# Softmax difference in the turned blocks instead of on VectorE, and unpadded queries

## The reference, cut to what matters

```python
def diff_attn(q, k, v, q_pos, k_pos, rel_bias, lam):
    ...
    a = probs(q[..., :DA_HEAD_DIM], k[..., :DA_HEAD_DIM]) - lam * probs(q[..., DA_HEAD_DIM:], k[..., DA_HEAD_DIM:])
    return jnp.einsum('bhqk,bkhd->bqhd', a.astype(v.dtype), v)

def peer(xn, w_q, sub_keys, u_tab, v_tab):
    ...
        act = jax.nn.gelu(jnp.einsum('td,thkd->thk', xb, u_tab[eidx]).astype(jnp.float32), approximate=False)
        return jnp.einsum('thk,thkd->td', (g * act).astype(xb.dtype), v_tab[eidx])
```

## Time and profile before

| | |
|---|---|
| median of 3 runs | 4118.31 us (4114.87 to 4126.76) |
| the profiled execution's own time | 4114.87 us |
| its span | 4113.1 us |
| PE / DVE / POOL / ACT busy | 68% / 62% / 55% / 26% |
| mean granted clock of PE | 0.748 of full speed |
| DMA, mean over the span | 338 GB/s |

### The profile page before, as it was taken

How to read it: one execution, slowest core, us unless ns; L and a number is a source line. 1 busy time by engine, 2 the same in 40 slices (tenths; PEclk the granted TensorE clock), 3 DMA queues, 4 the chain that set the end, 5 groups by cost and what they waited for, 6 DMA issues and landing times.

```text
span 4113.1 us, 50105 instructions
## 1 busy us (share of the span) xinstructions
PE 2803.7 (68%) x17164; PEld 1458.7 (35%) x17164; DVE 2543.0 (62%) x6861; ACT 1058.1 (26%) x2882; POOL 2270.1 (55%) x2365
## 2 busy tenths in 40 slices
PE   7889998677477757684768477758874754333365
PEld 6745544334243424342433243324442421000011
DVE  2445756766786677658776777688767556644400
ACT  3312212322232233222332233233322111110121
POOL 1102443665666566556666666566656656666665
PEclk9989999787678767786778678868875576555567
DMA  7635898999999999999999999999999999999998
GB/s 206 193 124 186 268 336 273 380 371 367 348 372 357 366 369 358 328 359 345 357 371 368 362 359 381 360 370 369 382 358 357 377 348 354 363 366 370 359 365 313
DMA packets 544250, 1389.51 MB, mean 338 GB/s; under 512 B 59496, under 2 KB 223776, under 8 KB 544000
## 3 DMA queue, kind: packets, MB, share of 16 engines
q0 software_dynamic: 335024, 1215.35, 79.0%
q1 hardware_dynamic: 196752, 161.33, 12.3%
q10 hardware_dynamic: 12224, 9.63, 0.8%
HBM read 1352.93 MB, written 33.04 MB: 337 GB/s over the span
## 4 chain that ended last, share of the span: by engine, by line
PE 16%; issue 14%; DMA 13%; POOL 11%; another core or an unknown queue 8%; DVE 7%; ACT 2%; SPq 1%; ACTq 0%; DVEq 0%; POOLq 0%
DMA d_vb<-in_peer_v_dram,d_eidT 6%; POOL d_vb L1686 5%; POOL d_ub L1667 5%; PE d_pY L1716 5%; DVE d_ub L1880 3%; DMA d_ub<-in_peer_u_dram,d_eid 2%; PE d_pS L842 2%; DMA r_side<-out_v_sample_dram 2%; PE r_pB L1432 2%; PE r_pB L1605 1%; PE d_pS L908 1%; PE d_pS L928 1%; DMA r_side<-scratch_hgT 1%; DMA t_shared<-scratch_kT 1%
## 5 line engine op out<-in xcount | busy, mean ns | idle before, releaser
L1880 DVE CUSTOM_DVE_ANT_0 d_ub<-d_ub,d_pX 128x1024 f32<-128x1024 f32 x1024 | 1240.7, 1217 | 630.1 <-DMA d_ub<-in_peer_u_dram,d_eid 516.0
L1667 POOL DMA_INDIRECT d_ub<-in_peer_u_dram,d_eid x1152 | 1133.8, 984 | 887.1 <-DVE d_hdot L1880 402.3
L1686 POOL DMA_INDIRECT d_vb<-in_peer_v_dram,d_eidT x1096 | 1053.5, 961 | 816.0 <-PE d_pY L1716 347.4
L1716 PE MATMUL d_pY<-d_vb,d_dg 128*32 128x256 f32 x8768 | 934.3, 514 | 829.4 <-DMA d_vb<-in_peer_v_dram,d_eidT 565.8
L1716 PEld LDWEIGHTS d_pY<-d_vb,d_dg 128*32 128x32 f32 x8768 | 260.1, 129 | 1405.3 <-issue 1197.4
L1755 ACT ACTIVATE d_dg<-c_late_sb,d_wgtT 128x32 f32<-128x32 f32 x1152 | 336.1, 315 | 1352.8 <-PE d_pY L1716 851.0
L704 PE MATMUL d_pX<-d_wq,d_vb 128*128 128x512 f32 (+3 forms) x1536 | 469.1, 458 | 16.0 <-DMA d_vb<-in_w_in_dram 8.5
L704 PEld LDWEIGHTS d_pX<-d_wq,d_vb 128*128 128x128 f32 x1536 | 269.4, 199 | 179.3 <-issue 112.2
L842 PE MATMUL d_pS<-t_shared,t_qz 128*128 128x512 f32 (+3 forms) x384 | 209.9, 680 | 52.9 <-DMA t_shared<-scratch_kT 31.9
L1880 DVE CUSTOM_DVE_ANT_0 d_ub<-d_ub,d_vb 128x1024 f32<-128x1024 f32 x128 | 155.4, 1221 | 44.6 <-DMA d_ub<-in_peer_u_dram,d_eid 43.8
L1432 PE MATMUL r_pB<-r_side,c_small_sb 128*128 128x128 f32 (+15 forms) x1152 | 170.5, 314 | 17.4 <-issue 13.4
(11 more groups left out here) (278 smaller groups left out, 3583.5 us busy)
## 6 DMA issues: line engine op xcount, KB each, us to landing
d_vb<-in_w_in_dram SPq DMA_DIRECT2D x68, 512.0 KB
d_ub<-in_peer_u_dram,d_eid POOLq DMA_INDIRECT x1152
d_vb<-in_peer_v_dram,d_eidT POOLq DMA_INDIRECT x1096
r_side<-in_cache_k_dram SPq DMA_DIRECT2D x16, 1024.0 KB
r_side<-in_cache_v_dram SPq DMA_DIRECT2D x16, 1024.0 KB
d_wo<-in_w_out_dram SPq DMA_DIRECT2D x6, 2048.0 KB, 9.1
d_wo<-in_peer_w_q_dram SPq DMA_DIRECT2D x4, 2048.0 KB, 8.8
scratch_h<-t_shared SPq DMA_DIRECT2D x9, 512.0 KB
```

Source lines behind the costliest of these rows:

```text
L1667: pool.indirect_dma_start(out=ub[:, g % R, :], out_offset=None, in_=io["peer_u"][0], in_offset=off).then_inc(u_in[g % R], 16)
L1686: pool.indirect_dma_start(out=to, out_offset=None, in_=io["peer_v"][0], in_offset=off).then_inc(landed, 16)
L1716: m = nc.tensor.matmul(pY[q * QT:(q + 1) * QT, g % 2, :], dg[:, n % DG, :], rows[:, q * QD:(q + 1) * QD], start=k % QT == 0, stop=k % QT = ...
L1880: nc.vector.tensor_tensor_reduce(out=ub[:, g % R, :], in0=ub[:, g % R, :], in1=xflat if i else xn_of(0), scale=1.0, scalar=0.0, op0=ALU.mu ...
```

## The change

Four things.

1. The maps are no longer joined on DVE. DVE makes two scaled identities, `mdg`, from coefficients 1 / Z0 and lambda-term / Z1. PE turns and joins in one: for each block and map a matmul with E as weights and `mdg` as the moving operand, two accumulated in PSUM. ACT's `output` has no scale. There is one `mdg`, so DVE waits for the turns of the unit before.
2. ACT's first exponential of a unit waits for all turns of the unit before and for `mdg_done`; its second waits for neither.
3. The queries come unpadded, one load of 256 KB for a tile ahead of the first keys, and the score matmuls take 32 rows of queries and keys. The fill of `qz` and SP's wait for `c_ready` go.
4. The scan's mask is a constant, `carry` ([128, 512], 256 KB more in the first load); both fills go.

```diff
     inchunk = (p[:, None] // SUB == np.arange(NSUB)[None, :]).astype(np.float32)
+    carry = np.tile((np.arange(W) % SUB != 0).astype(np.float32), (P, 1))
...
-        qz = ph.sb("t_qz", [P, 4, P])
...
+        mdg = ph.sb("t_mdg", [P, 2, P])
...
-            step(nc.vector.memset(qz[:], 0.0))
...
             if t:
-                if i == 0:
-                    sp.wait_ge(c_ready, 1)
+                sp.dma_start(qT, sc["qT"][t].rearrange("p (h n) -> p h n", h=4)).then_inc(in_q, 16)
                 for hp in range(4):
...
-                    for g in range(4):
-                        sp.dma_start(qz[32 * g:32 * g + 32, g, :], sc["qT"][t][32 * g:32 * g + 32, hp * P:(hp + 1) * P]).then_inc(in_q, 16)
...
+                r = 32 * (2 * h2 + m)
...
-                    ins = nc.tensor.matmul(pSf[:, at_bank[m] + a:at_bank[m] + a + n], qz[:, 2 * h2 + m, :], kTf[:, a:a + n], start=True, stop=True)
+                    ins = nc.tensor.matmul(pSf[:, at_bank[m] + a:at_bank[m] + a + n], qT[r:r + 32, hp, :], kTf[r:r + 32, a:a + n], start=True, stop=True)
...
             def turn(u, g):
-                pe.wait_ge(joined, turns[i] + ng * u + g + 1)
                 if g == 0:
+                    pe.wait_ge(mdg_done, U + u + 1)
...
-                    ins = nc.tensor.transpose(pT[:, (kb % TB) * P:(kb % TB + 1) * P], E[:, 1, kb * P:(kb + 1) * P], ident)
+                    for m in range(2):
+                        ins = nc.tensor.matmul(pT[:, (kb % TB) * P:(kb % TB + 1) * P], E[:, m, kb * P:(kb + 1) * P], mdg[:, m, :],
+                                               start=m == 0, stop=m == 1)
...
             def exps(u, m):
                 act.wait_ge(nmx_done, 2 * (U + u) + m + 1)
-                if U + u:
-                    act.wait_ge(T_psum if m else joined, turns[i] + ng * u)
+                if U + u and m == 0:
+                    act.wait_ge(T_psum, turns[i] + ng * u)
+                    act.wait_ge(mdg_done, U + u)
...
-                nc.scalar.activation(oa[:, u, :], pO[:, 0:VD], ACT.Copy, scale=share[u % 2][:, 0:1]).then_inc(o_done, 1)
+                nc.scalar.activation(oa[:, u, :], pO[:, 0:VD], ACT.Copy).then_inc(o_done, 1)
...
             def diagonals(u):
...
-                step(nc.vector.reciprocal(share[u % 2], Zs))
-                step(nc.vector.scalar_tensor_tensor(ratio, share[u % 2][:, 1:2], lam[:, 1:2], Zs[:, 0:1], ALU.mult, ALU.mult))
-                for g in range(ng):
-                    a, b = TB * g * P, min(TB * g + TB, nkb) * P
-                    nc.vector.scalar_tensor_tensor(E[:, 1, a:b], E[:, 1, a:b], ratio, E[:, 0, a:b], ALU.mult, ALU.add).then_inc(joined, 1)
+                    step(nc.vector.reciprocal(coef, Z[:, :, 1]))
+                step(nc.vector.tensor_tensor(coef, coef, lam[:], ALU.mult))
+                if U + u:
+                    dve.wait_ge(T_psum, turns[i] + ng * u)
+                nc.vector.tensor_tensor(mdg[:], ident[:, None, :].to_broadcast([P, 2, P]), coef[:, :, None].to_broadcast([P, 2, P]),
+                                        ALU.mult).then_inc(mdg_done, 1)
...
-            step(nc.vector.memset(flat(rl), 1.0))
-            step(nc.vector.memset(rl.rearrange("p h (c i) -> p (h c) i", i=SUB)[:, :, 0:1], 0.0))
...
-            nc.vector.tensor_tensor_scan(flat(rb), flat(rl), flat(re), 0.0, ALU.mult, ALU.add).then_inc(b_done, 1)
+            nc.vector.tensor_tensor_scan(flat(rb), carry, flat(re), 0.0, ALU.mult, ALU.add).then_inc(b_done, 1)
```

More of the change, by code:

```diff
@@ L82, in constants @@
     hot[:, QT - 1] = 1
-    small = np.concatenate([np.eye(P, dtype=np.float32), np.ones((P, P), np.float32), pick, block, inchunk,
+    small = np.concatenate([np.eye(P, dtype=np.float32), np.ones((P, P), np.float32), pick, block, inchunk, carry,
                             rows, second, places], axis=1)
@@ L90 @@
 _at = 0
-for _name, _w in (("ident", P), ("ones", P), ("pick", P + SUB - 1), ("block", P), ("inchunk", NSUB),
+for _name, _w in (("ident", P), ("ones", P), ("pick", P + SUB - 1), ("block", P), ("inchunk", NSUB), ("carry", W),
                   ("rows", 64), ("second", 1), ("places", NCAND)):
@@ L279, in layer @@
         Sc, E = ph.sb("t_S", [P, 2, NEARW]), ph.sb("t_E", [P, 2, SEQ])
+        mdg = ph.sb("t_mdg", [P, 2, P])
         st = ph.sb("d_st", [P, 4])
-        tiny, offset = ph.sb("t_tiny", [P, 16]), ph.sb("t_offset", [P, DH, 2])
-        mx, mxf, Zs = (tiny[:, 2 * n:2 * n + 2] for n in range(3))
+        tiny, offset = ph.sb("t_tiny", [P, 10]), ph.sb("t_offset", [P, DH, 2])
+        mx, mxf, coef = (tiny[:, 2 * n:2 * n + 2] for n in range(3))
         shift = tiny[:, 6:10].rearrange("p (m n) -> p m n", m=2)
-        share = [tiny[:, 10 + 2 * n:12 + 2 * n] for n in range(2)]
-        ratio = tiny[:, 14:15]
         Z = ph.sb("t_Z", [P, 2, 2])
@@ L300, in part @@
             return flat.rearrange(f"p ({' '.join(names)}) -> p {' '.join(names)}", **dict(zip(names, shape)))
-        kT, V, osq = part(shared, 512, NPT, P), part(shared, 1536, NPT, P), part(shared, 2560, DH, VD)
+        qT, kT, V, osq = part(shared, 0, 4, P), part(shared, 512, NPT, P), part(shared, 1536, NPT, P), part(shared, 2560, DH, VD)
         x = part(shared, 512, D)
@@ L345, in layer @@
         ident, places = small("ident"), small("places")
-        ones, pick, blockm, inchunk, rows_ = (small(n) for n in ("ones", "pick", "block", "inchunk", "rows"))
+        ones, pick, blockm, inchunk, carry, rows_ = (small(n) for n in ("ones", "pick", "block", "inchunk", "carry", "rows"))
         wo_in, wq_in, half_done = [ph.sem(f"d_wo_in{n}") for n in range(2)], ph.sem("d_wq_in"), ph.sem("d_half_done")
@@ L387, in layer @@
         s_psum, near_max, nmx_done, e_done = (ph.sem(n) for n in ("t_s_psum", "t_near_max", "t_nmx_done", "t_e_done"))
-        joined, T_psum, T_done, o_psum = (ph.sem(n) for n in ("t_joined", "t_T_psum", "t_T_done", "t_o_psum"))
+        mdg_done, T_psum, T_done, o_psum = (ph.sem(n) for n in ("t_mdg_done", "t_T_psum", "t_T_done", "t_o_psum"))
         o_done, osum, oroot, oa_done = (ph.sem(n) for n in ("t_o_done", "t_osum", "t_oroot", "t_oa_done"))
@@ L880, in mixer_tensor @@
             if t:
+                pe.wait_ge(in_q, 16 * (prompts[i] + 1))
                 pe_at = []
```

5 lines of the change are left out of this document (2 added, 3 removed).

## The result

The changed kernel takes 4184.62 us (median of 6 runs, 4164.06 to 4188.8) against 4117.83 us of the kernel before (6 runs, 4114.87 to 4137.4): ratio 1.0142, interval [1.0114, 1.0169]. It is slower by 1.4%, 67 us where 18 were forecast, and above the range that ended at 4172. The trace can show where those 40 us went, and not the rest.

What follows compares the result with a forecast made beforehand. PE was taken to bound 350 to 690 us and the gathers the time from 723 us on. Turns 8.3 + 14, scores 0.9, DVE and loads -6, start 0.8 gave +18 us: 4136 us, range 4110 to 4172.

Steps and rivals of the forecast that it cites:

- The bound: PE bounds 350 to 690 us; from 723 us on the gathers set the end, hiding most other engines' work.
- signs of being wrong: Tiles 6 to 8 not growing, attention clock moving over 0.05 with the rounds, or first stage's end moving over 16 us.
- The scores: 32-row score matmuls on PE: 14 ns more each, +0.9 us in tiles 1 and 2, bounds 0 and 3.
- Its fall was a rival: 32-row matmuls lower the clock where PE is the bound: 34 us if a tenth fell to half clock; chance 0.06.
- The later tiles' share: Extra time of the score matmuls after tile 2: 4.5 us, taken as inside PE's slack.
- The turns: Two fp32 matmuls per transpose on PE: +8.3 us in tiles 1 and 2, +14 us in tiles 3 to 8.
- rival B: All of PE's extra work is hidden from tile 3 on: +2 to +10 us, 4120 to 4128; chance 0.19.
- Rival E: Matmuls replacing transposes hold PE's clock at 2.4 GHz, so the turns pay for themselves, with rival B's result; chance 0.05.
- Rival C: PE becomes the pacer; 50 uncovered us and 10 for ACT's wait land whole: +55 to +70, 4173 to 4188; chance 0.12.
- The first stage: Stretch before the first V gather: about 5 us later at tile 2's end, 8 us in all.
- DVE and loads: Joins replaced by scaled identities on DVE, 33 us less busy, and keys asked for sooner: -6 us, bounds 0 and -32.
- rival D: DVE's saving and sooner keys matter more than PE: -22 us, 4096 to 4106; chance 0.12.

Runs made afterwards that it cites:

- e8: Kernel before with score matmuls reading only the 32 nonzero rows of the padded queries and the same key rows; loads and buffer kept: 1.0037.
- e9: Kernel before with score matmuls reading 64 rows, half of them zero in the queries; loads and buffer kept: 1.0054.
- e11: Kernel before with only ScalarE's first exponential of a unit waiting for the turns of the unit before, repeat of e3 on another chip: 1.001.
- e5: Changed kernel with padded queries, their loads and VectorE's mask fill put back; turns, scaled identities and waits stay changed: 1.0056.
- e15: Kernel before with one real matmul against the identity in place of each transpose: 1.0012.
- e14: Kernel before with two half-identity matmuls per block and ScalarE's first exponential waiting for the turns, joins kept; e4's kernel on a fourth chip: 1.0025.
- e3: Kernel before with only ScalarE's first exponential of a unit waiting for all turns of the unit before: 0.9981.
- e4: Kernel before with the edits of e2 and e3 together: two half-identity matmuls per block and ScalarE's changed wait: 1.0018.
- e2: Kernel before with each block turned by two matmuls against half the identity instead of one transpose, VectorE's join kept: 1.0031.
- e10: e4's kernel again, on the chip of e8 and e9, against the kernel before: 1.0022.
- e13: e5's kernel on a fourth chip: changed kernel with padded queries, their loads and VectorE's mask fill put back, against the kernel before: 1.0023.
- e6: Kernel before with unpadded queries, their single load per tile and the scan's mask from the constants, so all but the turns: 1.0035.
- e7: Kernel before with only the unpadded queries and their single load per tile, mask still filled on VectorE: 1.0054.
- e1: Changed kernel again on another chip, against the kernel before: 3945.35 us against 3913.06, ratio 1.0079.
- e12: Changed kernel again on a fourth chip, against the kernel before: 1.0071.

## Why the prediction was wrong

**The bound** was read rightly. From tile 3 on the gathers set the pace until PE's slack is used up; the rounds that grew by more than 3 us are those of tiles 7 and 8, with DMA shares of 0.96 and 0.95, and the one without attention stayed. They grew by 16.5 and 18.0 us, not by 3 to 7, and tile 6's not at all. One of the prediction's own signs of being wrong was met at tile 7: the clock of its attention stretch fell from 0.84 to 0.73 and its round grew.

**The scores are the step that failed.** Their term was +0.9 us, from 14 ns more for an instruction in a 64-row burst, with bounds of 0 and 3. Alone they cost 0.54% on the chip with 4121 us, 22 us with an interval of 13 to 31, and 0.37 to 0.54% elsewhere. The instruction's own time did not rise: 267/587/1218 ns against 272/592/1222. What rose was the time of all that follows on PE, in two ways.

The first is the change of shape. The burst of the earlier trace rows already held it, and it was misread: its 64-row matmuls start 112 ns apart, as full ones do, and the whole cost stands at its ends, 0.19 us at each. Of that its 2.05 us show 0.10; the rest of the difference to 1.82 comes from halving 3.64 us, which halves the last instruction's own time too. Spread over 16 instructions it looked like 14 ns each. The scores come in bursts of two to four, so a cost for each burst was priced as one for each instruction. In tiles 1 and 2 it measured 3.6 us (e8) to 7.5 us (e9), outside the bounds of 0 and 3. The Trainium skill's rule that changing the tiling mode drains TensorE (TensorEngine Tiling, Key Properties) warned against the same edit. The trace agrees, with 0.14 to 0.20 us where the shape changes.

The second is the clock. Its fall was a rival, with a chance of 0.06, and two things in that rival were wrong. It was looked for only in the stretch where PE is the bound, whose clock in fact stayed at 0.98. And it was argued down by 64-row matmuls in that same stretch, where PE is busy 332 of 340 us and the clock did not move whatever their rows were. The rounds where the clock moves between its two levels are the later ones, at 0.75 to 0.85, and e9 shows that there 64 rows lower it as much as 32. That row could bear no verdict on them. The later tiles' share, put at 4.5 us inside the slack, was priced at a clock that was taken to hold. How the cost of the scores divides between the clock and the change of shape no run separates. Of the 49 us by which the sum fell short on the median's scale, the scores' term explains some 21 and the saving of 6 us for VectorE and the loads, which did not come, another 6.

**The turns** were sized about rightly where they can be compared. The price of a block was forecast at 0.345 us more; in tile 8 of the changed kernel three blocks take
```profile
2806.54 1.60 PE L852 MATMUL d_pS<-t_mdg,t_E 128*128 128x128 f32 x12
```
against 0.55 us for three transposes in e11, both at full clock: 0.35 a block. Their terms were 8.3 + 14 = 22.3 us; alone, in e5, they cost 0.56%, 23 us with an interval of 14 to 32. On the chips near 3910 us it was 0.2%, some 9 us, nearer to rival B.

**Rival E**, that real matmuls in place of transposes raise the clock, was given 0.05, and the clock does rise: e15 and e14 show 0.817 and 0.853 for 0.795 in the attention stretches. The Trainium skill's rule that a transpose does not count as busy in the same way (TensorE: Matmul & The Clock Gate, Part 4) agrees with these rows. They don't prove it, since the real matmuls also keep PE busy longer. Its result, that the turns pay for themselves, did not come: e14's 1.0025 lies above 1.

**Rival C**, PE the pacer, 4173 to 4188 us, holds the time. Its price was built from 50 us of uncovered turns and 10 of ScalarE's new wait. The first is too much, since the turns alone cost 23, and the second was nothing (e3 and e11, and e4 beside e2). It met the number by luck, with another sum: some 23 us of turns and 22 of few-row scores, together 1.10%, against the 1.42% [1.14, 1.69] of the first measurement. The rest is within the intervals of the three. So this rival is not confirmed by its number.

**The first stage** ended 13.4 us later, with 10.0 forecast and 16 as the limit. It can't be told from chance: one and the same kernel (e4, e10, e14) ended it at 725.2, 730.8 and 731.9 us on three chips.

**DVE and loads**, -6 us: DVE is 42.6 us less busy (2500.4 for 2543.0) where 33 were forecast, and the wait for keys fell by 24. Neither shows in the time: e13, with fewer joins, equals e14, and rival D had nothing behind it. The mask from the constants was put at nothing; e6 against e7 is -0.2%, with intervals that overlap.

**What stays open.** The changed kernel costs 1.4% on one chip and 0.8 and 0.7% on two others, the turns 0.56% and 0.2%. The chips with the larger cost are those whose gathers are slower, and slower gathers should leave PE more slack, not less. Why the cost differs was not found. On the faster chips the profiled e1 loses its time in tiles 7 and 8, as shown above. In the profiled e12 no round stands out (tile 8's is 390.0 us, 394.7 in e11), but that execution, 3911 us, is the fastest of its six. The same holds of e8: its profiled execution, 3906.6 us, is its fastest, and its rounds are within 5 us of e11's, so where the 0.37% of its median is lost no trace shows. Nor do the runs say what it is about a few-row matmul that lowers the clock, only that 32 and 64 rows of the array do it and 128 rows of which 96 are zero do not. Whether the rows themselves do it or the pauses at the change of shape is open.

## What to carry to other kernels

Zero rows that fill a matmul's contraction up to 128 look like waste, but here they held TensorE's clock and spared it a change of shape: cutting them saved nothing on the instruction and cost 0.4 to 0.5% of the kernel. Before an edit to PE is priced, look at the granted clock of the stretch in which it falls: it stayed at 0.97 to 0.99 (350 to 690 us) and at 0.50 (the round without attention) with every edit here, while between 0.6 and 0.9 the kind of instruction moved it and with it the price of all its neighbours, so a row from a stretch of the first kind can't speak for the second. And take the change apart into edits that keep the instruction count, as e8 does, since the busy times of the whole don't show such a cause. A cost read off a burst is to be placed before it is multiplied: start to start, this one stood at the burst's ends and not in its instructions.

## What the runs showed of the hardware

- Score matmuls with 32 or 64 rows took as long as with 128 (587, 589 and 592 ns at the median) and lowered the mean granted clock from 0.758 to 0.734 and 0.736.
- A change between matmuls of shape 128\*128 and 32\*128 or 64\*128 delayed the next two starts by 0.14 to 0.20 us together at full clock (e8 and e9 against e11), and the durations don't show it. With 32 rows the matmuls of a head's two maps overlapped (0.70 us for four of 256 columns in e8), with 64 rows, at the same place in the array, they did not (1.13 us in e9).
- Real fp32 matmuls against an identity in place of transposes raised it, one to 0.764 and two to 0.774 from 0.757, at 0.53 us against 0.18 for a block turned at full clock (two matmuls, 1.60 us for three blocks; one transpose, 0.55 for three).
- The chips differ: the kernel before took 4118 and 4121 us in two of the five sets of runs, and 3907 to 3913 in the three others, on other chips. The round without attention took 367 to 369 us with 365 to 369 GB/s in the former, 333 to 334 us with 407 GB/s in the latter, window of e11:
```profile
3395.00:3724.00 329.00, 136.78 (x1010) 29.72 (x1010) 158.78 (x263) 43.70 (x133) 236.18 (x253) 0.50 1.03 407
```
